# Memory output of the final block by halves of the heads in four banks; two score steps moved ahead of turns and gates

## What is computed

```python
# 8 heads of 64, 2 key heads; branches: compressed, selected, window
z = h @ w_in[l]
b = nsa_attention(q, kv, gl, ...)            # scores, softmax, times values
x = x + mixed @ w_out[l]

def memory_cross_attention_2(h, mem, ...):   # 4 heads of 128
    q = rms_norm_2((h @ w_mq).reshape(B, T, 4, 128), q_g)
    s = jnp.einsum('bthd,bmhd->bhtm', q, k) * 128 ** -0.5
    p = jax.nn.softmax(s, axis=-1)
    o = jnp.einsum('bhtm,bmhd->bthd', p, v).reshape(B, T, 512)
    return o @ w_mo                          # 512 x 1024: "memory output"

x = x + memory_cross_attention_2(...)
h = rms_norm_2(x, norm_ffn_g[l])
x = x + jnp.square(jax.nn.relu(h @ w_ff1[l])) @ w_ff2[l]
```

## Time and profile before

| what | value |
|---|---|
| median of three executions | 1296.43 us (1294.35 to 1297.06) |
| the profiled execution | 1293.16 us |
| its span, first to last instruction | 1291.4 us |
| mean granted clock of TensorE | 0.989 |
| busy: PE, DVE, ACT, POOL | 1245.8, 809.6, 670.7, 92.7 us |
| load of 1 MB of `w_ff` weights, issue to landing | 5.3 us |

### The profile page before, as it was taken

The page is one execution under the profiler, slowest core; times in us unless marked ns, Lnnn a source line. Parts: engine busy times, 40 slices in busy tenths (PEclk is TensorE's granted clock), DMA queues, the critical chain, the costliest instruction groups (busy, mean ns, idle before and its releaser), DMA issues.

```text
span 1291.4 us, 23483 instructions
## 1 busy us (share of the span) xinstructions
PE 1245.8 (96%) x10259; PEld 1216.6 (94%) x10259; DVE 809.6 (63%) x921; ACT 670.7 (52%) x959; POOL 92.7 (7%) x65
## 2 busy tenths in 40 slices
PE   3999999999999999999999999999899998999998
PEld 2999999989999999999988999999889997999998
DVE  5478647666664477864666766446777875666542
ACT  5466546555544346664545564433566754565432
POOL 3000001020000000000202000001200110100000
PEclk8999999999999999999999999999989999999999
DMA  5733553346656634454333675665451442376552
GB/s 178 261 103 131 166 164 129 99 130 196 218 183 201 190 115 120 143 164 162 126 105 98 200 220 191 193 191 161 139 168 66 132 162 71 122 219 198 193 184 93
DMA packets 195572, 202.91 MB, mean 157 GB/s; under 512 B 5716, under 2 KB 191847, under 8 KB 195471
## 3 DMA queue, kind: packets, MB, share of 16 engines
q1 hardware_dynamic: 192704, 194.82, 47.4%
q0 software_dynamic: 2464, 5.99, 1.6%
q10 hardware_dynamic: 303, 0.61, 0.2%
HBM read 200.33 MB, written 3.16 MB: 158 GB/s over the span
## 4 chain that ended last, share of the span: by engine, by line
PE 88%; DVE 4%; ACT 3%; DMA 2%; issue 1%; POOL 1%; DVEq 0%; ACTq 0%; POOLq 0%
PE bank L576 15%; PE bank L578 14%; PE bank L577 14%; PE bank L2323 7%; PE bank L2321 7%; PE bank L2319 7%; PE bank L619 2%; PE bank L627 2%; PE bank L621 2%; PE bank L2236 2%; PE bank L2220 2%; DVE w_lo L536 1%; PE bank L2162 1%; POOL sumsq L766 1%; PE bank L2242 1%
## 5 line engine op out<-in xcount | busy, mean ns | idle before, releaser
L536 DVE TENSOR_TENSOR w_lo<-raw,w_hi 128x2048 fp32r<-128x2048 f32 (+7 forms) x210 | 424.7, 2032 | 325.5 <-ACT w_hi L526 325.1
L526 ACT ACTIVATE w_hi<-raw 128x2048 fp32r<-128x2048 f32 (+7 forms) x210 | 355.3, 1704 | 354.2 <-PE bank L2323 130.0
L576 PE MATMUL bank<-act_hi,w_hi 128*128 128x256 f32 (+1 forms) x1104 | 309.2, 280 | 0.0
L578 PE MATMUL bank<-act_hi,w_lo 128*128 128x256 f32 (+1 forms) x1104 | 306.3, 277 | 0.0
L577 PE MATMUL bank<-act_lo,w_hi 128*128 128x256 f32 (+1 forms) x1104 | 306.3, 277 | 0.0
L2319 PE MATMUL bank<-h_hi,w_hi 128*128 128x256 f32 x768 | 212.5, 277 | 0.0
L2323 PE MATMUL bank<-h_hi,w_lo 128*128 128x256 f32 x768 | 212.3, 276 | 0.0
L2321 PE MATMUL bank<-h_lo,w_hi 128*128 128x256 f32 x768 | 212.3, 276 | 0.0
L576 PEld LDWEIGHTS bank<-act_hi,w_hi 128*128 128x128 f32 (+1 forms) x1104 | 207.0, 187 | 0.9 <-issue 0.3
L577 PEld LDWEIGHTS bank<-act_lo,w_hi 128*128 128x128 f32 (+1 forms) x1104 | 207.3, 188 | 0.4
L578 PEld LDWEIGHTS bank<-act_hi,w_lo 128*128 128x128 f32 (+1 forms) x1104 | 206.8, 187 | 0.1
(11 more groups left out here) (380 smaller groups left out, 2109.6 us busy)
## 6 DMA issues: line engine op xcount, KB each, us to landing
raw<-in_w_up_dram SPq DMA_DIRECT2D x32, 1024.0 KB, 5.4
raw<-in_w_down_dram SPq DMA_DIRECT2D x32, 1024.0 KB, 5.2
raw<-in_w_ff_dram SPq DMA_DIRECT2D x32, 1024.0 KB, 5.3
raw<-in_w_in_dram SPq DMA_DIRECT2D x23, 1024.0 KB, 5.3
raw<-in_w_xk_dram SPq DMA_DIRECT2D x8, 1024.0 KB, 5.2
raw<-in_w_xv_dram SPq DMA_DIRECT2D x8, 1024.0 KB, 5.3
raw<-in_w_mix_out_dram SPq DMA_DIRECT2D x8, 1024.0 KB, 5.1
raw<-in_w_xq_dram SPq DMA_DIRECT2D x8, 1024.0 KB, 5.5
```

The lines of the kernel that those rows point to most:

```text
L526: ins = act.activation(d, r, ACT.Copy)
L536: ins = dve.tensor_tensor(d, r, h.bitcast(F32), ALU.subtract)
L576: pe.matmul(o, stat_hi, mov_hi, start=first, stop=False)
L578: return pe.matmul(o, stat_lo, mov_hi, start=False, stop=last)
```

## The change

It does four things. In PE's order, scores 4 moves ahead of turn 0, and scores 5 ahead of the gates' transpose and the first product with the values. Slabs 25 and 26 become four steps: `mhalf` 25 and 26 multiply head tiles 0 and 1 into all four banks, when `o_lo` is 5; `mrest` 25 and 26 add head tiles 2 and 3, when `o_lo` is 6, and signal the banks and the slabs. The two products for the clock ahead of slab 25 go. And the list of bank uses follows the new order. The programs of ACT, DVE, POOL and SP are as before.

```diff
-WARM_2 = {("pair", 0): ("y0", 4), ("hq", 6): ("hs6", 2), ("hb", 6): ("scores12", 3), ("scores", 12): ("scores12", 3),
-          ("slab", 25): ("mo0", 2)}
+WARM_2 = {("pair", 0): ("y0", 4), ("hq", 6): ("hs6", 2), ("hb", 6): ("scores12", 3), ("scores", 12): ("scores12", 3)}
...
-     ("scores", 0), ("scores", 1), ("scores", 2), ("cht", 1), ("scores", 3), ("slab", 9), ("turn", 0), ("turn", 1),
-     ("slab", 10), ("scores", 4), ("gt", 0), ("pv", 0), ("scores", 5), ("pv", 1), ("turn", 2), ("turn", 3), ("slab", 11),
+     ("scores", 0), ("scores", 1), ("scores", 2), ("cht", 1), ("scores", 3), ("slab", 9), ("scores", 4), ("turn", 0), ("turn", 1),
+     ("slab", 10), ("scores", 5), ("gt", 0), ("pv", 0), ("pv", 1), ("turn", 2), ("turn", 3), ("slab", 11),
...
-    + [("slab", 25), ("slab", 26), ("pair", 27), ("stat", 2)] + [("slab", s) for s in range(29, 51)]
+    + [("mhalf", 25), ("mhalf", 26), ("mrest", 25), ("mrest", 26), ("pair", 27), ("stat", 2)] + [("slab", s) for s in range(29, 51)]
...
-        elif kind in ("hb", "rest"):
+        elif kind in ("hb", "rest", "mrest"):
             pass
-        elif kind == "half":
+        elif kind in ("half", "mhalf"):
             uses += slab_banks_2(n)
...
+            def memory_half(s, half):
+
+                wh, wl = w_view(DEPTH, s, 512)
+                names = [u for u, _, _ in slab_banks_2(s)]
+                pe.wait_ge(sig["slab_lo"], v2("slab_lo", s + 1))
+                pe.wait_ge(sig["o_lo"], v2("o_lo", 5 + half))
+                for m in range(4):
+                    if m % 2 == 0:
+                        b = (bank if half else open_bank_2)(names[m // 2], DEPTH)
+                    c = slice(P * m, P * m + P)
+                    dst = b[:, T * (m % 2):T * (m % 2) + T]
+                    for k in (2 * half, 2 * half + 1):
+                        pe.matmul(dst, wh[:, k, c], o_hi[:, k], start=k == 0 and m % 2 == 0, stop=False, skip_group_check=True)
+                        pe.matmul(dst, wh[:, k, c], o_lo[:, k], start=False, stop=False, skip_group_check=True)
+                        ins = pe.matmul(dst, wl[:, k, c], o_hi[:, k], start=False, stop=k == 3, skip_group_check=True)
+                    if half and m % 2:
+                        ins.then_inc(sig["first_bank" if m == 1 else "slab_used"], 1)
...
-                elif s in (25, 26):
-                    wh, wl = w_view(DEPTH, s, 512)
-                    pe.wait_ge(sig["slab_lo"], v2("slab_lo", s + 1))
-                    pe.wait_ge(sig["o_lo"], v2("o_lo", 6))
-                    for m in range(4):
-                        if m % 2 == 0:
-                            b = open_bank(pe, DEPTH, names[m // 2])
-                        c = slice(P * m, P * m + P)
-                        for k in range(4):
-                            ins = products3(pe, b[:, T * (m % 2):T * (m % 2) + T], wh[:, k, c], wl[:, k, c],
-                                            o_hi[:, k], o_lo[:, k], k == 0, k == 3)
-                        if m % 2:
-                            ins.then_inc(sig["first_bank" if m == 1 else "slab_used"], 1)
```

More of the change, by code:

```diff
@@ L2419, in turn_gates, with open_bank_2 @@
                 ins.then_inc(once["gate_turned"], 1)
+            def memory_half(s, half):
[14 more added lines that the diff above has]
+                        ins.then_inc(sig["first_bank" if m == 1 else "slab_used"], 1)
+            def open_bank_2(use, layer):
+                return open_bank(pe, layer, use)
             def half_2(s):
@@ L2627, in pair_2 @@
                 slab_pair(pe, DEPTH, s, names, {0: 0, 23: 16, 27: 24}[s])
-            steps_2 = {"slab": slab_2, "pair": pair_2, "stat": stat_2, "gt": turn_gates, "half": half_2, "rest": rest_2, "hq": query_sums, "hs": head_sums, "hb": head_spread, "sgw": turn_token_weights, "cht": turn_hidden, "mem": turn_memory,
+            steps_2 = {"slab": slab_2, "pair": pair_2, "stat": stat_2, "mhalf": lambda s: memory_half(s, 0), "mrest": lambda s: memory_half(s, 1), "gt": turn_gates, "half": half_2, "rest": rest_2, "hq": query_sums, "hs": head_sums, "hb": head_spread, "sgw": turn_token_weights, "cht": turn_hidden, "mem": turn_memory,
                        "vturn": turn_compressed_values, "cscores": compressed_scores, "cturn": turn_compressed,
```

## The result

The changed kernel took **1305.26 us** (median of 6 executions, 1302.57 to 1306.49) against 1295.77 for the kernel before beside it (6 executions, 1294.35 to 1297.06): a ratio of 1.0064, 95% interval 1.0048 to 1.0081. Measured once more later, beside other executions of the kernel before, the ratio was 1.0048 (1.0033 to 1.0063). So it is slower, by 6.2 to 9.5 us, where 4.2 was forecast. Executions of this program scatter: 33 of the kernel before ran from 1292.85 to 1300.94 us in one comparison, 35 from 1291.95 to 1304.72 in another.

What follows compares the result with a forecast made beforehand. TensorE, busy for 96% of the span, was taken as the bound, so only its stalls and low clock count. Terms +1.7, +2.0 and +0.5 sum to +4.2 us: 1300.6 for the median, range 1297.2 to 1304.2.

Steps and rivals of the forecast that it cites:

- both waits: PE waits at turn 3 for DVE's mask addition of scores 4, and at pair 27 for DVE's part of slab 28.
- First place, turn 3: Turn 3 lands on scores 4's bank; PE stands from 951.9 until about 956.15, when DVE's addition has read it.
- the term of 1.7: Slab 11, behind the waiting turn 3, starts at 956.8 instead of 955.08: +1.7 us, low clock as before.
- The upper bound of +3.5: First place in all, if the low clock stretch of nearly 7 us begins only with slab 11.
- Second place, start: Memory output's first half needs only the first o_lo subtraction, so PE starts at 1096.17 instead of 1096.80: -0.6 us.
- pause before the pair: Pair 27 waits for slab 28's remainder from DVE, starting about 1109.77 instead of 1107.77: +2.0 us, start's gain included.
- act_lo, +0.5: Pair 27's third products wait for DVE's first act_lo product, slow beside POOL's addition: +0.5 us; 0 at median duration.
- Rival 1: The clock falls at the second place too, 3.3 us or more at 0.50, costing 1.7: 1302.3; chance 0.25.
- Rivals 2 and 4: 2: turn 3 does not wait, 1298.2, chance 0.10; 4: neither wait bites, semaphores met in another order, 1295.1, chance 0.07.
- Rival 3: Final block's low clock stretches vanish and pay the waits back, -0.8 in sum: 1295.6, not slower; chance 0.08.

Runs made afterwards that it cites:

- the unchanged kernel's other profile: The kernel before with no edit, run beside itself for a second profile: 1295.9 us, ratio 1.0004.
- slab by slab: Against halves alone: each slab's first and second half finished before the next slab; old scores order, no clock products: 1294.79 us, ratio 0.9986.
- waits filled: Changed kernel plus clock-keeping products, eight before turn 3 and five before pair 27: 1301.79 us, ratio 1.0047.
- halves alone: Kernel before with only the memory output by halves and without the two clock products; old scores order: 1300.33 us, ratio 1.0030.
- DVE's order alone: Kernel before with only DVE's mask additions of scores 4 and 5 moved ahead of the split of slab 12: 1297.46 us, ratio 1.0002.
- scores with DVE's mend: Against scores alone: DVE's mask additions of scores 4 and 5 moved ahead of the split of slab 12: 1294.24 us, ratio 0.9982.
- scores alone: Kernel before with only scores 4 and 5 moved in PE's order as in the change: 1300.59 us, ratio 1.0028.
- both mends: Changed kernel with DVE's mask additions of scores 4 and 5 ahead of slab 12's split, and halves finished slab by slab: 1295.09 us, ratio 0.9989.

## Why the prediction was right, and where it was short

**Direction and both waits: right.** The cause was read off the bank numbers and two queues before anything ran, and each mend that removes one wait removes its part's whole price (5.4 and 3.8 us in the profiles, 6.0 and 5.7 by the ratios).

**First place, turn 3: exact.** Forecast: start at 956.15, 11.23 us after slab 9's last matmul at 944.92. Measured: 962.14 - 950.90 = 11.24. Slab 11 started 12.00 us after that point (forecast 11.88). Turn 3 alone was a record group of 1.11 us; I had put half of the eight records' 1.91, 0.95.

**First place, the term of 1.7: mis-sized, +2.65.** The start of slab 11 accounts for 1.84 (12.00 against 10.16). The other 0.81 is slab 11 itself, 7.98 us instead of 7.17. I had taken "the like of before" for its low clock, 3.2 us of it; after the pause it was 5.0 (962.9 to 967.9). The upper bound of +3.5 holds it. Part of this is which profile stands for the kernel before: the same place took 15.82 us in the unchanged kernel's other profile, and against that one the changed kernel's 19.98 would be +4.2.

**Second place, start: right in kind, mis-sized.** PE starts the first half 0.10 us after the first part of o_lo. But its two subtractions started 1.33 us apart, as in the unchanged kernel's second profile, and not 0.7 as in the earlier trace rows. So PE started 2.11 us behind the last value product instead of 3.43: 1.3 us earlier, forecast 0.6. In the kernel with slab by slab, where the parts came together as in the earlier trace rows, the pair kept 0.6.

**Second place, pause before the pair: +2.0 forecast, +1.66 measured.** From the last value product to the pair it was 14.40 us in the profile before and 14.41 in the unchanged kernel's other one, 16.06 in the changed kernel and 15.82 in it again. From the start of the first half the pair was forecast after 13.60 us and came after 13.95 and 13.71. The step from half to first update took 7.34 us in the first of these, where matmuls came every 0.118 us, and 7.10 in the second, where they came every 0.114 as before; forecast 7.13. The remainder's end to PE took 0.25, not 0.1. The steps from update to ACT (0.73), and from split to remainder, are those forecast. The idle time was 2.41 and 2.58, forecast 2.6.

**act_lo, +0.5: hidden under another cost.** DVE's first product again ran slow beside POOL's addition (1.57 us, against a median of 0.48), the addition first, as forecast. But the clock fell at 1118.1, so that PE came to its third products later than the product was ready, and the stretch from pair to stat 2 took 12.80 us instead of 11.10: +1.70. Where the clock stayed at 1.00 (waits filled) it took 11.90. There the third products came 1.21 us behind the first ones instead of 0.91, so the stall itself was 0.3; the rest of the 0.8 is the wider spacing of the matmuls, and what the fall adds to it in the changed kernel is 0.9. The two differences, +1.66 and +1.70, make the +3.36.

**Rival 1, given 0.25, was what happened.** The clock fell within 1 us of the pair's start in each profiled kernel that had that pause unfilled (four of four) and in no other kernel at that place. The step that failed is the weighing: a pause of 2.1 us at full clock in the earlier trace rows was held against it. That row was one draw. The same pause, 2.0 to 2.2 us of waiting for a remainder, stands in all fourteen profiles. In six of them the clock fell within 0.6 us of its end (in the changed kernel at 940.6), in eight it stayed at 1.00. Length alone doesn't decide, then, and what does, no run shows. The Trainium skill ("TensorE: Matmul & The Clock Gate", section "Why this matters for your kernels") warns of idle gaps longer than the second pause here. With the first, of 3.97 us, the trace agrees; of the second's 2.41 us it gives no warning, and the clock fell all the same.

**Sum.** At the two places the profile has 2.65 + 1.66 + 1.70 = 6.0 us against 1.7 + 2.0 + 0.5 = 4.2 forecast; the second comparison has 6.2 (0.0048 of 1296). Rival 1's sum, 5.9, is nearer than its parts are: the first place was 0.9 dearer and the pause 0.3 cheaper. The first comparison's 9.5 puts the time 1.1 us above the range's end. The two comparisons of the same kernel lie 3 us apart, and the range had only 1.0 for that scatter. The 2.6 in the range's end should be 2.5, the 2.0 and 0.5 of the second place.

Rivals 2 and 4 needed turn 3 or the pair to run without a pause; both paused. Rival 3, the clock paying back, didn't occur: the mean granted clock was 0.980 to 0.985 in the six executions of the first comparison after the change, and 0.989 in the profile before.

## What to carry to other kernels

Where banks or buffers are handed out by position in a list, moving one step ahead renumbers every use behind it; write down the new neighbours eight places apart and ask where in the reader's own queue the release stands. Move the reader with the producer, or the move buys a wait (here 6 us between the two). When work is split in halves, finish first what the other engines' queues wait for, the first bank above all: the gain of an early start is kept only if nothing is handed on later than before.

## What the runs showed beside this

**One profile is one draw of the clock.** The first place of the kernels with PE's old order there took 17.33, 15.82, 15.82, 17.35 and 17.35 us (before, unchanged again, halves alone, slab by slab, DVE's order alone), with a granted clock of 0.80 or 0.89. Without the low stretches all of them would take about 14 us, by the estimate above. A fall that one profile shows at a place need not be at that place in the next, and a term of 1 to 2 us that rests on it is no more than a sample.

**The stretch ahead of the change differed, and why stays open.** In the six profiled executions with scores 4 at its old place, slab 9's last matmul stood at 944.4 to 946.4 us; in the eight with it moved, at 947.3 to 952.0, with the same 7466 instructions of PE before it. Most of it is falls of the clock near 270, 475, 900 and 935 us that the others mostly lack. The times speak against a cost of the kernel. The profiled executions of the first six were 1.4 to 3.3 us faster than their kernels' medians; those of the eight ranged from 1.9 faster to 5.6 slower. The scores with DVE's mend had 950.6 in its profile, which was the slowest of its 12 executions, and the lowest median of all kernels. No run here separates chance from a cause.

**The mean clock of all executions.** Each time comes with its granted clock. Half clock for a share of the span lowers the mean by half that share, so 0.001 in the mean is worth at most 1.3 us of 1300 (an estimate; less where PE stood idle meanwhile).

| kernel | ratio | mean clock, and of the kernel before beside it |
|---|---|---|
| scores alone | 1.0028 | 0.9845, 0.9878 |
| scores, DVE mended | 0.9982 | 0.9897, 0.9874 |
| halves alone | 1.0030 | 0.9861, 0.9878 |
| halves slab by slab | 0.9986 | 0.9880, 0.9874 |
| changed, again | 1.0048 | 0.9849, 0.9873 |
| changed, waits filled | 1.0047 | 0.9870, 0.9873 |
| both mends | 0.9989 | 0.9871, 0.9874 |

The gain of the scores with DVE's mend, 2.3 us, is no more than the 3.0 that its higher clock can be worth, so the order by itself isn't shown to gain there. With both mends the clock is that of the kernel before, and 1.4 us are gained, within the scatter.

**Two spacings at full clock.** The 96 matmuls of the memory output came every 0.114 us before and every 0.118 after, both at a granted clock of 1.00. It isn't the change: the same changed kernel had 0.114 when it was profiled again, and DVE's order alone, with PE's program as before, had 0.118. What sets it, no run shows; over 96 matmuls it is 0.3 to 0.4 us.
